# Light expert blocks: 512 columns of each full down slab multiplied in plain fp32 from the raw slot, the other 1536 split as before

## The chip, the core and the metric

The kernel runs on one core of one Trainium2 chip. The metric is the device time of one execution in microseconds (us), as the median of several runs. The engines that matter are TensorE (PE in the rows, PEld for its weight loads), VectorE (DVE), ScalarE (ACT), GpSimd (POOL), and SyncE (SP), whose queue issues the weight transfers.

## What is computed

A trunk of two encoder layers over 256 tokens of width 1024, all in float32. Each layer has a mixer (Hyena convolutions and differential attention) and a feed-forward part. The feed-forward part of layer 0 is a dense SwiGLU. That of layer 1 is a mixture of 8 experts of which each token uses 2:

```
def swiglu(x, w_gate, w_up, w_down):
    return (jax.nn.silu(x @ w_gate) * (x @ w_up)) @ w_down      # 1024 -> 2752 -> 1024

def moe_ffn(x, w_router, w_gate, w_up, w_down):
    logits = (xt @ w_router)
    top_val, top_idx = lax.top_k(logits, 2)
    ...                                    # tokens grouped by expert
    out = zeros.at[tok].add(expert_output * softmax(top_val))
```

The change touches the experts' `@ w_down` alone.

## The kernel before

Every weight is streamed from HBM once, in slabs of 128 partitions x 2048 float32 (1 MiB, 1.0486 MB). A slab passes through a pipeline. **SP** loads it into one of 6 raw slots (`RAW`). **ScalarE** copies it to `HI`, rounded to the reduced format float32r (line 768, `w_hi<-raw`). **VectorE** subtracts `HI` from the raw slab, which gives the remainder `LO` (line 1154, `w_lo<-raw,w_hi`). **TensorE** multiplies with `HI` and with `LO`, so that the sum is nearly a full float32 product. `HI` and `LO` have 3 slots each. The semaphores are `raw_loaded`, `hi_ready`, `lo_ready` and `slab_used`, each counting slabs in order. ScalarE splits slab n only when TensorE has used slab n-3. SP's queue is strictly in order: before each load it waits on `lo_ready` for the slab that had the same raw slot (line 591, in `put`), since after the subtraction nobody reads the raw slot any more.

The mixture of experts runs as blocks, one per expert, of 36 slabs each: slabs 0 to 3 are half slabs of gate and up weights (loaded in pairs), then come triples of two gate/up slabs and one down slab. Slabs 6, 9, ..., 33 are the full down slabs of a block, ten of them. Slabs 31 and 32 have 1536 columns, 34 has 1024 and 35 has 512. Blocks 0, 1, 3, 5 and 7 are heavy: up to 96 tokens, three multiplications for each piece of weight (high tokens by `HI`, low tokens by `HI`, high tokens by `LO`; lines 1723, 1724, 1990, 2013). Blocks 2, 4 and 6 are light: up to 64 tokens, of which the high part and the remainder stand side by side as 128 columns of the stationary operand, so that two multiplications do (lines 2069 and 2075 for gate/up, 2100 and 2107 for down). The rows 64 to 127 of the result then hold the product of the token remainders; `lo_copy` (line 1004) and `add_lo` (line 2081) bring them to the other rows.

In a light block each triple runs so. ScalarE: `turned_hi_light` (line 1016, the turned activations of the last chunk to float32r), split of the first slab, `lo_copy`, split of the second, `silu`, split of the down slab. VectorE: subtraction of the first slab, `mult_light` (line 1535, the product `act`), subtraction of the second, `turned_lo_light` (line 1545, the remainder of the activations), subtraction of the down slab. TensorE: gate/up slab, the transposes of `act` (`turn_act_light`, line 2088), gate/up slab, `down_light`, `add_lo`.

## Time and profile before

| what | value |
|---|---|
| median of 3 runs | 1379.55 us (1376.91 to 1380.21) |
| the profiled execution's own time | 1375.47 us |
| its span | 1373.6 us |
| granted TensorE clock, mean share of full speed | 0.998 |
| TensorE, VectorE, ScalarE busy | 95%, 83%, 64% of the span |
| read from HBM | 376.36 MB |

The profile is of one execution. Busy time is that of recorded instructions; a matmul's record covers its whole passage through the array, and records of successive matmuls overlap, so the distance between starts is the cost of one in a series. In a table of stretches the columns are the stretch and its length, then busy us of PE, PEld, DVE, ACT and POOL, the granted clock, the DMA share (mean busy share of 16 DMA engines) and GB/s. The mixture of experts fills the second half of the span, from about 640 us on; its three light blocks lie at about 840 to 922, 1015 to 1096 and 1187 to 1270 us.

### The profile page before, as it was taken

To read this page: it belongs to the slowest core of one execution; us is meant where nothing else is said; L and a number is where in the kernel's file an instruction comes from. 1 tells how busy PE (TensorE), PEld (TensorE's weight loads), DVE (VectorE), ACT (ScalarE), POOL (GpSimd) and SP (SyncE) were. 2 spreads that over 40 slices of the span, in tenths; PEclk is the share of its full clock that TensorE was granted. 3 is DMA by queue.
4 is the path that set the end of the run, shared out by engine and by line. 5 is a ranking of instruction groups with operands and counts; after the bars stand their busy time and mean duration, and the time that the engine had idled before them with its cause. 6 is when DMAs were issued, how large, how long until landed. Compare 5 with 4: busy or idle time off the path is not lost.

```text
span 1373.6 us, 17422 instructions
## 1 busy us (share of the span) xinstructions
PE 1311.0 (95%) x6156; PEld 982.4 (72%) x6156; DVE 1143.5 (83%) x1233; ACT 878.1 (64%) x965; POOL 81.0 (6%) x64
## 2 busy tenths in 40 slices
PE   6999989999999999999999999999999999999998
PEld 3887768888887887678667676666766667666675
DVE  5988787654447989875998988999889998899998
ACT  4345644544434445635776777987779877798775
POOL 0011010000000020010051000000000000000400
PEclk9999999999999999999999999999999999999999
DMA  7444333975483344152899999999999999999996
GB/s 293 180 157 150 123 137 138 337 288 184 172 345 120 152 153 153 62 207 92 320 364 382 414 360 372 404 405 422 380 365 411 402 422 386 364 406 401 421 395 256
DMA packets 63564, 394.67 MB, mean 287 GB/s; under 512 B 6914, under 2 KB 7486, under 8 KB 23818
## 3 DMA queue, kind: packets, MB, share of 16 engines
q1 hardware_dynamic: 58778, 375.37, 70.2%
q10 hardware_dynamic: 2848, 11.53, 2.1%
q0 software_dynamic: 1872, 6.91, 1.5%
q8 instruction: 38, 0.62, 0.2%
q14 instruction: 28, 0.23, 0.0%
HBM read 376.36 MB, written 17.43 MB: 287 GB/s over the span
## 4 chain that ended last, share of the span: by engine, by line
PE 70%; DVE 21%; issue 5%; ACT 3%; DVEq 0%; DMA 0%; SPq 0%; POOL 0%; ACTq 0%
PE bank L1723 15%; PE bank L1724 15%; DVE w_lo L1154 14%; PE bank L2013 13%; PE bank L1990 9%; PE bank L1773 5%; ACT w_hi L768 2%; PE bank L1768 2%; PE bank L1894 2%; PE bank L1736 1%; DVE ys L1143 1%; PE bank L1887 1%; PE bank L2000 1%; DVE act L1535 1%; PE bank L2107 1%
## 5 line engine op out<-in xcount | busy, mean ns | idle before, releaser
L1154 DVE TENSOR_TENSOR w_lo<-raw,w_hi 128x2048 fp32r<-128x2048 f32 (+2 forms) x383 | 794.1, 2089 | 94.0 <-ACT w_hi L768 92.7
L768 ACT ACTIVATE w_hi<-raw 128x2048 fp32r<-128x2048 f32 (+2 forms) x383 | 669.4, 1755 | 131.2 <-PE bank L2013 58.5
L1723 PE MATMUL bank<-w_hi,hT_hi 128*128 128x512 f32 (+3 forms) x968 | 382.5, 395 | 2.8 <-DVE hT_lo L1143 1.8
L1724 PE MATMUL bank<-w_hi,hT_lo 128*128 128x512 f32 (+3 forms) x968 | 375.1, 388 | 0.0
L1723 PEld LDWEIGHTS bank<-w_hi,hT_hi 128*128 128x128 f32 (+1 forms) x968 | 170.2, 176 | 51.7 <-issue 4.8
L1724 PEld LDWEIGHTS bank<-w_hi,hT_lo 128*128 128x128 f32 (+1 forms) x968 | 170.3, 176 | 44.8 <-issue 1.0
L1990 PE MATMUL bank<-w_lo,hT_hi 128*96 128x512 f32 (+3 forms) x616 | 162.3, 388 | 0.8 <-DVE w_lo L1154 0.8
L1990 PEld LDWEIGHTS bank<-w_lo,hT_hi 128*96 128x96 f32 (+1 forms) x616 | 103.1, 169 | 37.4 <-DVE w_lo L1154 4.3
L1773 PE MATMUL bank<-w_lo,hT_hi 128*128 128x512 f32 x352 | 87.5, 391 | 0.0
L2075 PE MATMUL bank<-w_lo,hT_hi 128*128 128x512 f32 (+1 forms) x264 | 78.2, 414 | 9.1 <-DVE w_lo L1154 9.1
L967 ACT ACTIVATE act_hi<-bank 128x192 fp32r<-128x192 f32 (+1 forms) x66 | 24.7, 375 | 94.8 <-PE bank L2000 94.8
L2013 PE MATMUL bank<-w_hi,act_lo 128*96 128x512 f32 (+1 forms) x294 | 78.8, 394 | 1.9 <-DVE act_lo L1495 1.8
L2013 PE MATMUL bank<-w_hi,act_hi 128*96 128x512 f32 (+1 forms) x294 | 78.5, 393 | 0.8 <-ACT act_hi L967 0.8
L2013 PE MATMUL bank<-w_lo,act_hi 128*96 128x512 f32 (+1 forms) x294 | 78.0, 391 | 0.0
L1773 PEld LDWEIGHTS bank<-w_lo,hT_hi 128*128 128x128 f32 x352 | 65.8, 188 | 13.9 <-issue 0.4
L2069 PE MATMUL bank<-w_hi,hT_hi 128*128 128x512 f32 (+1 forms) x264 | 74.4, 400 | 0.2
L2075 PEld LDWEIGHTS bank<-w_lo,hT_hi 128*128 128x128 f32 x264 | 44.5, 188 | 36.5 <-DVE w_lo L1154 31.2
L2013 PEld LDWEIGHTS bank<-w_hi,act_lo 128*96 128x96 f32 (+1 forms) x294 | 48.8, 169 | 22.7 <-DVE act_lo L1495 6.4
L2013 PEld LDWEIGHTS bank<-w_lo,act_hi 128*96 128x96 f32 (+1 forms) x294 | 49.6, 169 | 17.7
L2013 PEld LDWEIGHTS bank<-w_hi,act_hi 128*96 128x96 f32 (+1 forms) x294 | 49.2, 169 | 17.4 <-issue 1.0
L2069 PEld LDWEIGHTS bank<-w_hi,hT_hi 128*128 128x128 f32 x264 | 46.9, 188 | 10.9 <-ACT w_hi L768 1.5
L1495 DVE TENSOR_TENSOR act_lo<-bank,act_hi 128x192 fp32r<-128x192 f32 (+1 forms) x66 | 26.9, 407 | 28.4 <-ACT act_hi L967 28.3
(281 smaller groups left out, 1347.9 us busy)
## 6 DMA issues: line engine op xcount, KB each, us to landing
raw<-in_moe SPq DMA_DIRECT2D x240, 1024.0 KB, 7.9
raw<-in_mix SPq DMA_DIRECT2D x56, 1024.0 KB, 4.9
raw<-in_dense SPq DMA_DIRECT2D x30, 1024.0 KB, 4.9
raw<-in_moe SPq DMA_DIRECT2D x16, 768.0 KB, 8.4
raw<-in_moe SPq DMA_DIRECT2D x12, 512.0 KB, 7.4
slot_h<-x_squared ACTq DMA_DIRECT2D x1, 5632.0 KB, 43.0
slot_y<-x_squared ACTq DMA_DIRECT2D x1, 5632.0 KB, 24.2
raw<-in_moe SPq DMA_DIRECT2D x8, 256.0 KB, 5.4
```

The lines of the kernel that those rows point to most:

```text
L768: nc.scalar.activation(HI[:, split_slot, 0:width], RAW[:, raw_slot, half:half + width], ACT.Copy)\
L1154: vec.tensor_tensor(LO[:, split_slot, 0:width], RAW[:, raw_slot, half:half + width], HI[:, split_slot, 0:width].bitcast(F32), ALU.subtract ...
L1495: vec.tensor_tensor(R["act_lo"][:, :, 0:tbs * rows], turn_bank(layer, parity)[:, 0:2 * tbs * rows].rearrange("p (k t) -> p k t", k=2), R[" ...
L1723: mm(out_, left[0], right[0], start=start, stop=False)
L1724: mm(out_, left[1], right[1], start=False, stop=False)
L1768: ins = mm(bank(step, m)[:, 0:T], w_lo, HTH[:, kd, :], start=False, stop=sp_)
L1773: ins = mm(bank(step, tb)[:, :], HTH[:, kd, tok], w_lo, start=False, stop=sp_)
L1894: ins = mm(dst[:, :], DFT[:, 0, ri, par, :], src, start=True, stop=True)
L1990: ins = mm(gate_up_bank(tb, parity)[0:rows, 0:2 * width], HTH[:, kd, tok], w_lo, start=False, stop=kd == KD - 1)
L2013: ins = mm(PS[4 + 2 * tb + half][0:rows, :], left[0:h, k, tok], right[0:h, s, at:at + 512], start=first and k == 0, stop=last and k == 1)
L2069: mm(PS[parity][:, 0:2 * width], HTH[:, k0 + k, 0:2 * LCAP], w_hi, start=k0 + k == 0, stop=False)
L2075: ins = mm(PS[parity][:, 0:2 * width], HTH[:, k0 + k, 0:2 * LCAP], w_lo, start=False, stop=k0 + k == KD - 1)
```

## The change

In light blocks the last 512 columns (1536 to 2047) of each full down slab are no longer split. ScalarE and VectorE split only the first 1536 (`SPLIT_PART`). TensorE multiplies the last 512 straight from the raw slot in plain float32, with an unsplit copy of the turned activations (`ACT_WHOLE`, 64 columns) that ScalarE now makes ahead of the float32r copy. In `down_light` three of the four pieces remain in the `HI` group and in the `LO` group; the plain multiplication stands behind the `HI` group, ahead of the wait for `lo_ready`. As TensorE now reads the raw slot too, SP waits on `slab_used` instead of `lo_ready` before it loads into a slot that held such a slab; this also holds where the next load is that of the following heavy block. Nothing changes in heavy blocks otherwise, and the transfers are the same in number, size and order.

```diff
 LIGHT = 3
+LIGHT_BLOCKS = tuple(2 * i + 2 for i in range(LIGHT))
 PAIR = CAP + LCAP
...
 LATE_SLAB = 19
+LIGHT_DOWN = range(6, 34, 3)
+SPLIT_PART = SLAB - 512
 REJOINED = (LATE_SLAB - 2 + RAW_SLOTS, LATE_SLAB - 1 + RAW_SLOTS)
...
     FSP = sb("filters", [P, 2, 2, 2, 512])
+    ACT_WHOLE = SQUARES[:, 0:LCAP]
     HG = FSP[:, 0].rearrange("p a b c -> p a (b c)")
...
     def _(sp):
-        def put(slot, dst, src, free):
+        def put(slot, dst, src, free, multiplied=False):
             if free is not None:
-                sp.wait_ge(lo_ready, free)
+                sp.wait_ge(slab_used if multiplied else lo_ready, free)
             sp.dma_start(dst, src).then_inc(raw_loaded[slot], 16)
+
+        def follows_whole(b, p, late=False):
+
+            before = p - back(p, late)
+            return isinstance(b, int) and before % FFN_SLABS in LIGHT_DOWN and b + before // FFN_SLABS in LIGHT_BLOCKS
...
-            def two_halves(e, b, p, n):
+            def two_halves(e, b, p, n, multiplied=False):
...
                 put(slot, RAW[:, slot, :].rearrange("p (h n) -> p h n", h=2),
-                    blocks[e, at].rearrange("o (h p n) -> p (o h) n", h=2, p=P), n - back(p % FFN_SLABS) + 1)
-
-            def slab(e, b, p, n, late):
+                    blocks[e, at].rearrange("o (h p n) -> p (o h) n", h=2, p=P), n - back(p % FFN_SLABS) + 1, multiplied)
+
+            def slab(e, b, p, n, late, multiplied=False):
...
                     put(slot, RAW[:, slot, cols], blocks[e, at].rearrange("o (p n) -> p (o n)", p=P)[:, cols],
-                        None if i else n - back(p, late) + 1)
+                        None if i else n - back(p, late) + 1, multiplied)
...
                 for p in (0, 2):
-                    two_halves(e, at, p, n0 + p)
+                    two_halves(e, at, p, n0 + p, layer == 1 and follows_whole(b, p))
                 for i in range(4):
                     for j in range(6):
-                        slab(e, at, 4 + 6 * i + j, n0 + 6 * i + 4 + j, at == NE - 1 and 4 + 6 * i + j >= LATE_SLAB)
+                        part = 4 + 6 * i + j
+                        late = at == NE - 1 and part >= LATE_SLAB
+                        slab(e, at, part, n0 + part, late, layer == 1 and follows_whole(b, part, late))
                     if i == 0 and (y_at or y_light_at):
...
                         sp.dma_start(TOK_HEAVY[0:tok_heavy_at[1], :], slot_h[bass.ds(*tok_heavy_at), :]).then_inc(tok_heavy_loaded, 16)
-                    slab(e, at, p, n0 + p, at == NE - 1)
+                    slab(e, at, p, n0 + p, at == NE - 1, layer == 1 and follows_whole(b, p, at == NE - 1))
...
-            def turned_hi_light(q):
+            def turned_hi_light(q, whole=True):
                 act.wait_ge(turned, q + 1)
+                if whole:
+                    nc.scalar.activation(ACT_WHOLE, PS[2][:, CAP:CAP + LCAP], ACT.Copy)
                 nc.scalar.activation(R["act_hi"][:, :, 0:LCAP], PS[2][:, 0:2 * CAP].rearrange("p (k t) -> p k t", k=2)[:, :, 0:LCAP], ACT.Copy)\
...
                 silu_light(qb, k0, 0)
-                ffn_split(6, b, n0, r0)
+                ffn_split(6, b, n0, r0, SPLIT_PART)
...
                     silu_light(q, k, parity)
-                    ffn_split(p + 5, b, n0, r0)
+                    ffn_split(p + 5, b, n0, r0, SPLIT_PART)
...
                 ffn_split(35, b, n0, r0, D // 2)
-                turned_hi_light(qb + NCH)
+                turned_hi_light(qb + NCH, False)
                 turned_tokens_hi(b + 1, CAP)
...
                 mult_light(qb, 0)
-                ffn_split(6, b, n0)
+                ffn_split(6, b, n0, SPLIT_PART)
                 turned_lo_light(qb)
...
                     turned_lo_light(q)
-                    ffn_split(p + 5, b, n0)
+                    ffn_split(p + 5, b, n0, SPLIT_PART)
...
-            def down_light(n, s, q, start, tiles=(0, 1), amid=None):
-
+            def down_light(n, s, q, start, tiles=(0, 1), amid=None, whole=None):
+
+                parts = [(j, k, half) for j, k in enumerate(tiles) for half in range(2)][:4 if whole is None else 3]
                 pe.wait_ge(act_hi_ready, q + 1)
...
                 pe.wait_ge(hi_ready, n + 1)
-                for j, k in enumerate(tiles):
-                    for half in range(2):
-                        at = j * D + half * 512
-                        mm(PS[4 + half][:, :], R["act_hi"][:, k, 0:2 * LCAP], HI[:, s, at:at + 512], start=start and k == 0, stop=False)
+                for j, k, half in parts:
+                    at = j * D + half * 512
+                    mm(PS[4 + half][:, :], R["act_hi"][:, k, 0:2 * LCAP], HI[:, s, at:at + 512], start=start and k == 0, stop=False)
+                if whole is not None:
+                    mm(PS[5][0:LCAP, :], ACT_WHOLE, RAW[:, whole % RAW_SLOTS, SPLIT_PART:SLAB], start=False, stop=False)
                 if amid:
...
                 pe.wait_ge(lo_ready, n + 1)
-                for j, k in enumerate(tiles):
-                    for half in range(2):
-                        at = j * D + half * 512
-                        ins = mm(PS[4 + half][:, :], R["act_hi"][:, k, 0:2 * LCAP], LO[:, s, at:at + 512], start=False, stop=False)
+                for j, k, half in parts:
+                    at = j * D + half * 512
+                    ins = mm(PS[4 + half][:, :], R["act_hi"][:, k, 0:2 * LCAP], LO[:, s, at:at + 512], start=False, stop=False)
                 ins.then_inc(slab_used, 1)
...
                             pe.wait_ge(y_taken, 2 * b + 2)
-                        down_light(n0 + p + 2, slot(p + 2), q - 1, opening)
+                        down_light(n0 + p + 2, slot(p + 2), q - 1, opening, whole=block_place(layer, b, p + 2))
                         add_lo(k0 + 1 + j, 1 - j)
...
                 gate_up_light(n0 + 29, slot(29), 4, 4, CHUNK, 1)
-                down_light(n0 + 30, slot(30), q - 1, False)
+                down_light(n0 + 30, slot(30), q - 1, False, whole=block_place(layer, b, 30))
                 add_lo(k0 + NCH - 1, 1)
...
                 gate_up_light(n0 + 32, slot(32), 4, 4, TAIL, 0)
-                down_light(n0 + 33, slot(33), q, False, amid=lambda: add_lo(k0 + NCH, 0, TAIL))
+                down_light(n0 + 33, slot(33), q, False, amid=lambda: add_lo(k0 + NCH, 0, TAIL),
+                           whole=block_place(layer, b, 33))
                 turn_act_light(q + 1)
...
                 down_light(n0 + 34, slot(34), q + 1, False, tiles=(0,))
```

## Rows read from the trace of the kernel before

**Rows 1.** The page, busy us, share of the span and instructions of each engine.

```profile
PE 1311.0 (95%) x6156; PEld 982.4 (72%) x6156; DVE 1143.5 (83%) x1233; ACT 878.1 (64%) x965; POOL 81.0 (6%) x64
```

**Rows 2.** Stretches of blocks 2, 6 and 3; busy us, clock, DMA share, GB/s.

```profile
868.00:889.00 21.00, 19.52 (x81) 13.55 (x80) 21.00 (x16) 19.87 (x19) 0.00 (x0) 1.00 1.01 423
1237.00:1258.00 21.00, 19.45 (x80) 13.44 (x79) 21.00 (x16) 19.77 (x18) 0.00 (x0) 1.00 1.01 421
945.00:966.00 21.00, 21.00 (x96) 14.79 (x95) 18.80 (x14) 14.99 (x14) 0.00 (x0) 1.00 1.01 421
```

**Rows 3.** VectorE in order of time, block 2: start us, us, instruction.

```profile
866.29 4.48 DVE L1154 TENSOR_TENSOR w_lo<-raw,w_hi 128x2048 fp32r<-128x2048 f32 x2
870.69 0.41 DVE L1535 TENSOR_TENSOR act<-silu,bank 64x256 f32<-64x256 f32 x1
871.02 2.28 DVE L1154 TENSOR_TENSOR w_lo<-raw,w_hi 128x2048 fp32r<-128x2048 f32 x1
873.23 0.28 DVE L1545 TENSOR_TENSOR act_hi<-bank,act_hi 128x128 fp32r<-128x128 f32 x1
873.43 4.48 DVE L1154 TENSOR_TENSOR w_lo<-raw,w_hi 128x2048 fp32r<-128x2048 f32 x2
```

**Rows 4.** ScalarE in order of time, block 2.

```profile
872.22 0.28 ACT L1016 ACTIVATE act_hi<-bank 128x128 fp32r<-128x128 f32 x1
...
908.45 0.25 ACT L1016 ACTIVATE act_hi<-bank 128x128 fp32r<-128x128 f32 x1
```

**Rows 5.** ScalarE's waits from 886 to 911 us: total us, times, longest.

```profile
ACT w_hi L768 <- DMA raw<-in_moe: 0.8, 2, 0.4
```

**Rows 6.** Groups by form, the whole span: count, busy us, mean ns.

```profile
L1154 DVE TENSOR_TENSOR w_lo<-raw,w_hi 128x2048 fp32r<-128x2048 f32 x308 | 699.2, 2285 | 79.7 <-ACT w_hi L768 78.9
...
L1154 DVE TENSOR_TENSOR w_lo<-raw,w_hi 128x1536 fp32r<-128x1536 f32 x18 | 31.5, 1752 | 4.3 <-ACT w_hi L768 4.3
...
L768 ACT ACTIVATE w_hi<-raw 128x2048 fp32r<-128x2048 f32 x308 | 587.8, 1913 | 127.2 <-PE bank L2013 57.5 <-PE bank L1773 42.3 <-PE bank L1768 23.5
...
L768 ACT ACTIVATE w_hi<-raw 128x1536 fp32r<-128x1536 f32 x18 | 26.7, 1482 | 0.1
```

**Rows 7.** TensorE at slab 30 of block 2, in order of time.

```profile
910.28 1.08 PE L2100 MATMUL bank<-w_hi,act_hi 128*128 128x512 f32 x4
911.64 1.19 PE L2107 MATMUL bank<-w_lo,act_hi 128*128 128x512 f32 x4 [0.28 <-DVE w_lo L1154]
912.67 0.39 PE L2081 MATMUL bank<-lo_sum,swap 128*128 128x512 f32 x1
```

**Rows 8.** Plain float32 matmuls at the end of the span.

```profile
1366.26 3.67 PE L2234 MATMUL bank<-y_spread,spread_T 96*128 96x512 f32 x8 [0.78 <-ACT y_spread L1115]
```

**Rows 9.** VectorE, then TensorE, at slab 6 of block 2.

```profile
850.78 2.28 DVE L1154 TENSOR_TENSOR w_lo<-raw,w_hi 128x2048 fp32r<-128x2048 f32 x1
...
854.52 1.07 PE L2107 MATMUL bank<-w_lo,act_hi 128*128 128x512 f32 x4
```

**Rows 10.** Single loads: issue, us to landing; slabs 12, 13, 14, block 6's first.

```profile
L591 SPq DMA_DIRECT2D raw<-in_moe x1: 333/333/333, 853.2 to 853.2; - x1
DMA to landing us min/median/max: 6.8/6.8/6.8
...
L591 SPq DMA_DIRECT2D raw<-in_moe x1: 332/332/332, 855.9 to 855.9; - x1
DMA to landing us min/median/max: 6.6/6.6/6.6
...
L591 SPq DMA_DIRECT2D raw<-in_moe x1: 333/333/333, 859.2 to 859.2; - x1
DMA to landing us min/median/max: 7.4/7.4/7.4
...
L591 SPq DMA_DIRECT2D raw<-in_moe x1: 397/397/397, 1175.1 to 1175.1; - x1
DMA to landing us min/median/max: 5.0/5.0/5.0
```

## The prediction

> **What bounds the kernel now.** Start with the busy shares of the page [rows 1]: TensorE 95% and VectorE 83% of the span. These are averages over stages, so the second view is the table of stretches [rows 2]. It shows two regimes inside the expert stage. In a heavy block TensorE is busy 21.00 of 21.00 us while VectorE has 18.80. In a light block it is the other way round: VectorE is busy for 21.00 or almost 21.00 us of 21, TensorE for about 19.5. All three stretches have one thing in common, a DMA share of 1.01 at 421 to 423 GB/s, whether the block consumes quickly or slowly. One slab is 1.0486 MB, so at 422.5 GB/s, about the middle, a slab lands every 2.48 us and three slabs take 7.45 us.
>
> The third view is VectorE in order of time in the first light block [rows 3]. One period of three slabs (gate/up, gate/up, down) starts with a w_lo subtraction at 866.29 and ends with the next at 873.43: 7.14 us. From start to start the two subtractions take 4.40 us (2.20 each), the product `act` 0.33, the third subtraction 2.21 and the remainder of the token copy 0.20: 7.14 again. So VectorE runs without a gap, and this is what the change shortens. But 7.14 us is less than the 7.45 that the transfers need: the light block already eats the ring of raw slots faster than it is filled, 0.31 us per period. The ring's lead is gone before the block ends: at 886 to 911 us ScalarE, which splits first, waits for landings (0.8 us in two waits of 0.4) [rows 5]. In the last third of a light block transfers and VectorE are level, and behind the transfers there is nothing to win.
>
> **The change part by part.** *Subtraction.* A down slab of 2048 columns costs 2.21 us, one of 1536 columns 1.752 against 2.285 in single durations [rows 6]: 0.53 less, 10 slabs in 3 blocks, 16.0 us of VectorE time. A period would go from 7.14 to 6.61 us if VectorE set it. The transfers need 7.45. So this gain is spent on the ring running out earlier (0.84 us per period instead of 0.31), and what survives is only the distance between the last landings and the end of the block.
>
> *ScalarE.* The copy to w_hi goes from 1.913 to 1.482 us [rows 6], minus 0.43. The new copy ACT_WHOLE (128x64) has no row; the token copy of 128x128 takes 0.25 to 0.28 [rows 4], so it is between 0 and 0.28; I take 0.2, near that row, for half its columns. The period of ScalarE falls by some 0.2 and stays below 7.45. Cost nothing; if the transfers did not cover it, 30 x 0.2 = 6 us, less the 13 that the shorter copies give.
>
> *TensorE.* Per down slab one w_hi and one w_lo multiplication of 512 columns go, and a plain fp32 one comes. Four fp32r ones from 910.28 to 1.08 us later, each 0.39 long, are 0.23 apart [rows 7]. Eight records of plain fp32 of 512 columns take 3.67 us with 0.59 for the last one [rows 8]: 0.44 apart, and one fp32 matmul of the code leaves two records (four calls, eight records). So plain fp32 costs 0.88 against 2 x 0.23 = 0.46: TensorE gets 0.42 us of work per down slab. A period has 19.5/21 of busy time by the records [rows 2], but it waits for w_lo in each group, so there is room for the sum. Where it stands matters: the fp32 matmul lies before `lo_ready`. Now the w_hi group of slab 30 starts at 910.28 and the w_lo group at 911.64, 1.36 later, when the subtraction is done [rows 7]. After: three of 0.23 plus 0.88 = 1.57, so w_lo can't start before 911.85; three instead of four save 0.23 behind it, and `add_lo` at 912.67 comes at about 912.5. The subtraction is 0.53 sooner, but TensorE takes back some 0.3. At the end of a light block I count 0.33 gained, 1.0 for three; the bounds are 0 (TensorE takes back all) and 1.1 per block (the last two down slabs, nothing taken back), 3.2 in all.
>
> *The slots.* Ten raw slots of a light block are released by `slab_used` instead of `lo_ready`, and SP waits in order. In the middle of a block this is about 0.9 us later (three w_lo matmuls and their end, 1.2 us for four [rows 7]) less the 0.53: harmless, since loads already take 6.6 to 7.4 us around slab 12 [rows 10] and more when the ring's lead is used up, so that several are queued. At the opening it is not small. The subtraction of slab 6 is done at 853.06, SP issues slab 12 at 853.2 [rows 9, 10]. TensorE finishes slab 6 only at 854.52 + 1.07 = 855.59 [rows 9]. The new w_hi group starts 0.53 sooner and lasts 0.65 longer, the w_lo group is 0.23 shorter, so slab 12 is issued at about 855.6, 2.4 later. Slab 12 landed at 853.2 + 6.8 = 860.0 [rows 10], the one before it a spacing earlier, 857.5. The lead of issue over the previous landing falls from 4.3 to 1.9 us. What lead is enough? Lower bound: the shortest latency of such a load in these rows is 5.0 us [rows 10], minus 2.5 of transfer, a lead of 2.5; then a hole of 0.6. Upper bound: slab 14, issued at 859.2, landed at 866.6, 4.1 after slab 13 (855.9 + 6.6 = 862.5) [rows 10]. It had a lead of 3.3 and still left a hole of 1.6, so a lead of 4.9 is needed; then slab 12 leaves 3.0. Slabs 12 and 13 are loaded before that old hole of 1.6, which takes up a delay of that size, as slab 14 is released by slab 8 as before. What comes through is 0 to 1.4 us per block. I take the middle, 0.7, and 2.1 for three blocks; nothing behind hides it, because the rest of the block is at the transfer rate.
>
> The Trainium skill ("DMA: Bandwidth & Descriptors", Latency and other measured facts) puts the fixed cost of a DMA at about 2 us. By it the hole would be about 0.1 instead of 0.6 to 3.0, and the sum would fall below zero by the 1.0 gained; the 1.6 hole of slab 14 does not fit it.
>
> The same page (Where 436 GB/s comes from) puts the ceiling at 435 GB/s. By it three slabs would take 7.23 us, still more than 6.61, and each of some ten periods would have 0.2 us more to give; the trace never shows more than 423 in these stretches.
>
> *Heavy blocks behind.* Slab 30 gates the next block's first load the same way, up to 1 us later. TensorE sets the pace there, 21.00 of 21.00 us, with VectorE 2.2 us in hand over the stretch [rows 2], so I cost it at nothing; uncovered it would be 3 x 1 us. Arithmetic and volume of transfers are otherwise unchanged.
>
> Sum: -1.0 + 2.1 = +1.1 us on the profiled execution's 1375.47 (span 1373.6): 1376.6. The median of the runs is 4.08 above that execution, so 1380.6.
>
> **The rivals.** *VectorE is the bound throughout*: its gapless row speaks for it, the share of 1.01 and ScalarE's waits for landings against. 30 x 0.53 = 16.0 us, 1363.6. Chance 0.06.
>
> *The transfers lose their holes*: if the 1.6 us hole at slab 14 comes from VectorE being late and not from the queue, a faster VectorE closes it in three blocks: 4.8 + 1.0 = 5.8 us less, 1373.8. For it speaks that slab 14's load waits for the late subtraction of slab 8; against it, that a lead of 3.3 us is more than the 2.5 of the shortest load. Chance 0.15.
>
> *Slower, through the late release at the opening*: lead 1.9 us at slab 12. If 4.9 is needed and the old hole at slab 14 does not absorb (it moves along), 3.0 per block, 9.0 in all less 1.0 gained: 1387.6. With absorption and no gain at the end, +4.2. It decides from a needed lead of some 4.5 us on. Chance 0.23 for over 0.3%.
>
> *Nothing measurable* (the forecast's case, -3 to +4 us): 0.56.
>
> **How the numbers follow.** 0.3%, 4.1 us, is about what a measurement of this kernel can tell from no change. Faster: 0.06 + 0.15 = 0.21; same 0.56; slower 0.23. The likeliest case's own range is 1377 to 1384. Taking in the closed holes and most of the late release gives 1373 to 1387, with some 0.2 outside: the full VectorE gain, the full 9 us, and what I have not seen.
>
> **What would show it.** Right: w_lo of the down slabs 1.75 us, DMA share still 1.0 at some 422 GB/s in the middle of light blocks, VectorE now with gaps there, and more waits of ScalarE for landings, and from the middle of the block on instead of its last third; there periods of 7.45 us. Right for the slots: slab 12 of a light block issued 2.4 us later, with a slower landing. Wrong: periods of 6.6 us through the block, or more than 430 GB/s; or, on the other side, waits of TensorE in the heavy blocks, or the granted clock falling below 1.00 in light blocks [rows 2].

## The result and the profile after

The changed kernel takes 1385.26 us (median of 8 runs, 1382.05 to 1386.98). The kernel before, run beside it, takes 1379.88 (median of 8; one of them took 1846.83 us and is left out of the ratio; the others have a median of 1379.55). The ratio is 1.0042 with a 95% interval of 1.0030 to 1.0053: **slower by 0.42%, 5.8 us**. It lies inside the range of 1373 to 1387, but outside the likeliest case's own range of 1377 to 1384, and it has the sign and size of the slower rival. The profiled execution took 1385.68 us, span 1383.8.

Ratios below are against the kernel before, run on the same chip; 0.001 is 1.38 us, and each ratio is uncertain by 0.001 to 0.002.

The page, in the form of [rows 1]:

```profile
PE 1328.7 (96%) x6156; PEld 982.8 (71%) x6156; DVE 1129.1 (82%) x1233; ACT 872.1 (63%) x995; POOL 80.4 (6%) x64
```

VectorE lost 14.4 us of work and TensorE gained 17.7. The stretch of block 2 answers to [rows 2]:

```profile
868.00:889.00 21.00, 20.56 (x81) 13.19 (x80) 19.62 (x16) 18.98 (x22) 0.00 (x0) 1.00 0.99 400
```

The clock is still 1.00. TensorE is now busy for 20.56 us of 21 where it had 19.52, and VectorE, gapless before, has 19.62. VectorE in order of time, block 2, beside [rows 3]:

```profile
867.24 2.28 DVE L1167 TENSOR_TENSOR w_lo<-raw,w_hi 128x2048 fp32r<-128x2048 f32 x1
...
869.64 3.94 DVE L1167 TENSOR_TENSOR w_lo<-raw,w_hi 128x1536 fp32r<-128x1536 f32 x2
874.05 0.41 DVE L1548 TENSOR_TENSOR act<-silu,bank 64x256 f32<-64x256 f32 x1 [0.46 <-ACT silu L1022]
874.39 2.28 DVE L1167 TENSOR_TENSOR w_lo<-raw,w_hi 128x2048 fp32r<-128x2048 f32 x1
```

The two subtractions went from 4.48 to 3.94 us, the 0.53 that was promised. But from 867.24 to 874.39 the period is 7.15 us, where it was 7.14: the time came back as a gap of 0.46 us before `act`, waiting for `silu`. Nothing of the saving is left, and that already at 870 us, where transfers don't yet hold anything back. The chain of waits says who holds it:

```profile
867.24 2.29 DVE w_lo L1167
...
869.57 1.21 PE bank L2088 x4
870.78 0.69 PE bank L2113 x3
871.48 1.00 PE bank L2115 x2
872.48 0.89 PE bank L2121 x3
873.37 0.24 PE bank L2094
...
873.64 0.39 ACT silu L1022
...
874.05 0.06 DVE act L1548
874.10 0.28 issue
874.39 2.29 DVE w_lo L1167
```

This is a closed loop, and each turn is one period: the w_lo subtraction of a gate/up slab, its w_lo matmuls (L2088), the down slab's w_hi matmuls (L2113), the plain multiply (L2115, 1.00 us), the down slab's w_lo matmuls (L2121), `add_lo` (L2094), `silu`, `act`, and the next subtraction. Before the change the same loop held two more float32r matmuls of 0.23 us [rows 7] and no plain multiply, so it was about 7.15 - 1.00 + 0.46 = 6.6 us long, half a microsecond under the 7.14 of VectorE, and didn't show.

The forms answer to [rows 6] and [rows 8]:

```profile
L1167 DVE TENSOR_TENSOR w_lo<-raw,w_hi 128x1536 fp32r<-128x1536 f32 x48 | 83.5, 1745 | 4.3 <-ACT w_hi L779 4.3
...
L2115 PE MATMUL bank<-raw,squares 128*64 128x512 f32 x60 | 32.2, 618 | 0.0
```

ScalarE's waits for landings, 886 to 911 us, beside [rows 5]:

```profile
ACT w_hi L779 <- DMA raw<-in_moe: 2.2, 3, 1.0
```

The loads of slabs 12, 14 and 18 of block 2 (issue, us to landing; the first two answer to [rows 10]), and then slab 18 before the change:

```profile
L595 SPq DMA_DIRECT2D raw<-in_moe x1: 333/333/333, 859.2 to 859.2; - x1
DMA to landing us min/median/max: 4.8/4.8/4.8
...
L595 SPq DMA_DIRECT2D raw<-in_moe x1: 333/333/333, 862.6 to 862.6; - x1
DMA to landing us min/median/max: 6.4/6.4/6.4
...
L595 SPq DMA_DIRECT2D raw<-in_moe x1: 333/333/333, 873.5 to 873.5; - x1
DMA to landing us min/median/max: 7.3/7.3/7.3
```

```profile
L591 SPq DMA_DIRECT2D raw<-in_moe x1: 333/333/333, 868.7 to 868.7; - x1
DMA to landing us min/median/max: 7.8/7.8/7.8
```

Read them against the block's own start. VectorE's subtraction of slab 6 starts at 854.03 after and at 850.78 before [rows 9], so the profiled block begins 3.25 us later. The code ahead of it is the same; at least part of this is TensorE's clock, which was granted at its lower level (0.50, 1.2 GHz) for 6.8 us each from 184.3 and from 426.7 us on in the execution after, and for 3.4 us each from 424.8 and from 643.3 on in the one before. Less 3.25, slab 12 is issued at 855.95 (before 853.2: 2.75 late) and lands at 860.75 (860.0: 0.75 late). Slab 14 lands at 865.75 (866.6: 0.85 early). Slab 18 is issued at 870.25 (868.7: 1.55 late) and lands at 877.55 (876.5: 1.05 late). So the delay at the opening is swallowed by the old hole at slab 14, and a new one arises at slab 18, in the middle of the block. From the end of slab 12's subtraction to the issue of slab 18's load there are 2.15 us, where there were 0.17. Measured from slab 6's subtraction, slab 24 lands 0.86, 1.44 and 1.16 us later than before in the three blocks: 3.5 us together.

**Where the time is lost in the trace.** The light blocks can be timed by themselves, from VectorE's subtraction of slab 6 to that of slab 4 of the next block. For block 2 the first line is the end of that stretch before (its start is in [rows 9]), the others are its start and end after:

```profile
927.98 2.29 DVE L1154 TENSOR_TENSOR w_lo<-raw,w_hi 128x2048 fp32r<-128x2048 f32 x1
```

```profile
854.03 1.74 DVE L1167 TENSOR_TENSOR w_lo<-raw,w_hi 128x1536 fp32r<-128x1536 f32 x1
...
933.20 2.29 DVE L1167 TENSOR_TENSOR w_lo<-raw,w_hi 128x2048 fp32r<-128x2048 f32 x1
```

That is 77.2 us before and 79.2 after; the three blocks together take 231.3 and 238.1, 6.7 more. The two stretches between them, each nearly a whole heavy block, take 97.1 us before and after. Of the 6.7 us, 2.7 are lost at the ends of the blocks: from the subtraction of slab 30 to that of the next block's slab 4 it takes 19.56, 19.57 and 19.66 us where it took 18.66, 18.66 and 18.75. The largest step there is from slab 33's subtraction to slab 34's, 3.8 us instead of 2.8.

### The profile page after: what moved, and what is told of

Read it like the earlier page. It is cut to its first block, busy times and chain, and to the rows that moved or that the text cites. A ratio compares the mean times of both kernels' runs of the same rounds, so it can differ in the third digit from the quotient of the medians.

```text
span 1383.8 us, 17452 instructions
## 1 busy us (share of the span) xinstructions
PE 1328.7 (96%) x6156; PEld 982.8 (71%) x6156; DVE 1129.1 (82%) x1233; ACT 872.1 (63%) x995; POOL 80.4 (6%) x64
## 4 chain that ended last, share of the span: by engine, by line
PE 75%; DVE 15%; ACT 5%; issue 3%; DMA 1%; SPq 0%; POOL 0%; DVEq 0%; ACTq 0%
PE bank L1736 15%; PE bank L1737 15%; PE bank L2026 13%; DVE w_lo L1167 9%; PE bank L2003 8%; PE bank L1786 5%; ACT w_hi L779 3%; PE bank L2088 3%; PE bank L1781 2%; PE bank L1749 2%; PE bank L1907 1%; DVE ys L1156 1%; DMA raw<-in_moe 1%; PE bank L2115 1%; PE bank L1900 1%
## 5 line engine op out<-in xcount | busy, mean ns | idle before, releaser
L1167 DVE TENSOR_TENSOR w_lo<-raw,w_hi 128x2048 fp32r<-128x2048 f32 (+2 forms) x383 | 778.7, 2047 | 97.2 <-ACT w_hi L779 95.5
L779 ACT ACTIVATE w_hi<-raw 128x2048 fp32r<-128x2048 f32 (+2 forms) x383 | 657.4, 1722 | 141.0 <-PE bank L2026 56.4
L2088 PE MATMUL bank<-w_lo,hT_hi 128*128 128x512 f32 (+1 forms) x264 | 75.9, 405 | 10.8 <-DVE w_lo L1167 9.6
L2088 PEld LDWEIGHTS bank<-w_lo,hT_hi 128*128 128x128 f32 x264 | 46.0, 188 | 34.4 <-DVE w_lo L1167 27.5
L2026 PEld LDWEIGHTS bank<-w_lo,act_hi 128*96 128x96 f32 (+1 forms) x294 | 49.6, 169 | 17.7
```

The costliest lines, as they stand in the source:

```text
L779: nc.scalar.activation(HI[:, split_slot, 0:width], RAW[:, raw_slot, half:half + width], ACT.Copy)\
L1167: vec.tensor_tensor(LO[:, split_slot, 0:width], RAW[:, raw_slot, half:half + width], HI[:, split_slot, 0:width].bitcast(F32), ALU.subtract ...
L2026: ins = mm(PS[4 + 2 * tb + half][0:rows, :], left[0:h, k, tok], right[0:h, s, at:at + 512], start=first and k == 0, stop=last and k == 1)
L2088: ins = mm(PS[parity][:, 0:2 * width], HTH[:, k0 + k, 0:2 * LCAP], w_lo, start=False, stop=k0 + k == KD - 1)
```

## The experiments

**The change in four parts.** Four kernels make a square: with and without the shorter split, the plain multiply and the late release. In `late_release_alone` the arithmetic is that of before and only SP's wait is changed. In `early_release` the plain multiply reads a resident tile instead of the raw slot, so the slot is free at `lo_ready`; the product is of other data. `no_plain_multiply` and `split_less_alone` leave the product over the last 512 columns of the light blocks' down slabs out.

```diff
# late_release_alone, in the kernel before (with follows_whole as in the change)
-                sp.wait_ge(lo_ready, free)
+                sp.wait_ge(slab_used if multiplied else lo_ready, free)
# early_release, in the changed kernel
-                sp.wait_ge(slab_used if multiplied else lo_ready, free)
+                sp.wait_ge(lo_ready, free)
-                    mm(PS[5][0:LCAP, :], ACT_WHOLE, RAW[:, whole % RAW_SLOTS, SPLIT_PART:SLAB], start=False, stop=False)
+                    mm(PS[5][0:LCAP, :], ACT_WHOLE, X[:, 0, 0:512], start=False, stop=False)
# no_plain_multiply: the line mm(PS[5]...) taken out
# split_less_alone: that, and sp.wait_ge(lo_ready, free)
```

> The kernel before, in which only SP's waits for the ten down slabs of each light block are changed from lo_ready to slab_used; no column is treated differently, the output is unchanged. Theory A (the late release leaves holes in the transfers) expects +3 to +6 us against the kernel before, holes at slab 12, at slab 18 and at the next block's first load, and later landings at the end of light blocks. Theory B (the cost is the plain multiplication in TensorE's chain) expects within 1 us of the kernel before. If VectorE's saving matters at all, this one is slower than the changed kernel.

> The changed kernel, with SP waiting on lo_ready as before; so that this is free of races, the plain multiplication reads 512 columns of the residual stream instead of the raw slot (512 columns of each full down product in light blocks are therefore of other data). Same instructions and sizes on every engine. Theory A: most of the loss is gone, -1 to +2 us against the kernel before; what stays is the tail of light blocks, where slab 34 comes 0.9 us later per block. Theory B: +4.5 to +6, as the changed kernel.

> The changed kernel without the plain fp32 multiplication (512 columns of each full down slab of light blocks are left out of the product); the late release stays, but slab_used comes 0.9 us sooner. Theory A: the lead at slab 12 is 0.9 us longer, so about half of the holes stay, +1 to +3 us against the kernel before. Theory B: the loss is gone, -3 to 0.

> The changed kernel with neither the plain multiplication nor the late release (512 columns of each full down slab of light blocks are left out of the product). It shows what 16 us less of VectorE and 13 us less of ScalarE are worth by themselves. If the transfers bound the light blocks as forecast, -1 to -4 us against the kernel before. If VectorE bounds them, -12 to -16 us.

| kernel | split cut | plain multiply | late release | ratio (95%) | us |
|---|---|---|---|---|---|
| late_release_alone | no | no | yes | 1.0024 (1.0012 to 1.0036) | +3.3 |
| early_release | yes | yes | no | 1.0018 (1.0008 to 1.0028) | +2.5 |
| no_plain_multiply | yes | no | yes | 0.9982 (0.9969 to 0.9994) | -2.5 |
| split_less_alone | yes | no | no | 0.9957 (0.9942 to 0.9972) | -5.9 |
| the change | yes | yes | yes | 1.0042 (1.0030 to 1.0053) | +5.8 |

By these ratios the parts add up. Late release: +3.3 alone, 5.8 - 2.5 = +3.3 with the plain multiply, -2.5 + 5.9 = +3.4 without it. Plain multiply: 2.5 + 5.9 = +8.4 with the early release, 5.8 + 2.5 = +8.3 with the late one. Shorter split: -5.9. Sum: -5.9 + 8.4 + 3.3 = +5.8.

Against what was expected: `late_release_alone` is within theory A's +3 to +6. `early_release` lies between A's -1 to +2 and B's +4.5 to +6, since each theory held one of two causes for the whole. `no_plain_multiply` is within B's -3 to 0, and `split_less_alone` lies between the -1 to -4 for transfers as the bound and the -12 to -16 for VectorE.

The three light blocks in the profiled executions (one each; the three blocks of the kernel before agree within 0.2 us) give the same order, but smaller sizes for two parts:

| kernel | three light blocks, us | against before |
|---|---|---|
| before | 231.3 | 0 |
| late_release_alone | 236.6 | +5.3 |
| early_release | 234.4 | +3.1 |
| no_plain_multiply | 231.7 | +0.4 |
| split_less_alone | 228.3 | -3.0 |
| the change | 238.1 | +6.7 |

The shorter split is worth 3.0 us here, not 5.9, and the plain multiply costs 6.1 to 6.3, not 8.4. Part of the gap is TensorE's clock in other stages: the six runs of `split_less_alone` had a mean granted clock of 0.9968, the 29 of the kernel before beside them 0.9948, and over all runs of the kernel before that are on record a run is about 0.9 us shorter for each 0.001 more. By this estimate some 2 us of the 5.9 have nothing to do with the edit. The late release costs 3.4 to 3.7 us in the two pairs with the shorter split. Alone it shows 5.3, of which 2.8 stand between slabs 6 and 12 of blocks 2 and 6; there the clock was granted at 0.50 (1.2 GHz) for 3.4 us, from 856.2 and from 1207.8 on, after TensorE had been busy for 3.45 of 6.2 us and for 3.88 of 6.8. Without these 2.8 it is 2.5.

With neither the plain multiply nor the late release the period is 6.87 us, not the 6.61 that VectorE alone would allow. VectorE of `split_less_alone` in order of time, then ScalarE:

```profile
867.03 2.27 DVE L1167 TENSOR_TENSOR w_lo<-raw,w_hi 128x2048 fp32r<-128x2048 f32 x1
...
873.56 0.41 DVE L1548 TENSOR_TENSOR act<-silu,bank 64x256 f32<-64x256 f32 x1 [0.19 <-ACT silu L1022]
873.90 2.28 DVE L1167 TENSOR_TENSOR w_lo<-raw,w_hi 128x2048 fp32r<-128x2048 f32 x1
```

```profile
870.59 0.59 ACT L1015 ACTIVATE lo_sum<-bank 64x512 fp32r<-64x512 f32 x1 [0.42 <-PE bank L2088]
871.21 1.92 ACT L779 ACTIVATE w_hi<-raw 128x2048 fp32r<-128x2048 f32 x1
```

This is a second loop. The subtraction that starts at 867.03 feeds four matmuls, ScalarE's `lo_copy` waits 0.42 us for them (870.59), then comes a whole w_hi copy (1.92), then `silu`, `act` at 873.56 and the next such subtraction at 873.90. It is 6.87 us long, so 0.27 of VectorE's 0.53 can't come out.

**Where the plain multiply stands.** `own_semaphore` gives the plain multiply a semaphore of its own, so that SP needn't wait for the w_lo group behind it. `plain_between_groups` also moves it ahead, between the w_hi and the w_lo group of the gate/up slab before (at a block's first down slab it stays). `plain_after_add` moves it behind `add_lo` instead, in the eight middle down slabs of each block; the first and the last are split whole.

```diff
# own_semaphore
-                sp.wait_ge(slab_used if multiplied else lo_ready, free)
+                sp.wait_ge(lo_ready, free)
+                if multiplied:
+                    sp.wait_ge(whole_used, multiplied)
...
+                        .then_inc(whole_used, 1)
# plain_between_groups, beside that: passed to gate_up_light as amid
+            def whole_between(n, q, place):
+                pe.wait_ge(act_hi_ready, q + 1)
+                pe.wait_ge(hi_ready, n + 1)
+                down_whole(place)
# plain_after_add, beside that
                         add_lo(k0 + 1 + j, 1 - j)
+                        if not opening:
+                            down_whole(block_place(layer, b, p + 2))
```

> The changed kernel, with the late release mended and the output intact: the plain multiplication counts a semaphore of its own, and SP waits on lo_ready and on that one instead of slab_used. As the multiplication stands before the w_lo group, it is over when the subtraction is or up to 0.9 us later. If late release and plain multiplication add up, as in the runs so far, +2 to +3.5 us against the kernel before, like the run with early release. Rival: the release was not what counted there but the other data read by TensorE (the raw slot is being read while transfers write next to it); then +5 to +6.

> As own_semaphore, and the plain multiplication moves ahead: between the w_hi and the w_lo group of the gate/up slab before, where TensorE waits 0.2 to 0.5 us for VectorE (the first down slab of each block stays as it is). If the cost of the plain multiplication is that it lies in the loop w_lo of gate/up, w_hi of down, plain, w_lo of down, add_lo, silu, act, subtraction (7.13 us in the changed kernel's chain, 6.2 without the plain one), the period falls to about 6.9 us until the transfers run out, and the time to -3 to -6 us against the kernel before, close to the run without the plain multiplication. If the cost is TensorE's work as such, it stays at +2 to +3.

> The plain multiply of a down slab is issued behind the addition of the low part instead of ahead of it, with a semaphore of its own for the slot's release, in the eight middle slabs of each light block; slabs 6 and 33 are split whole as before the change. If the loop through the addition and silu is what the multiply lengthens, it is now out of it: the period falls towards the 6.87 us of the kernel without the multiply, and the time is 1 to 4 us under the kernel before. If the slot's later release (about 1.8 us behind the split) costs what that takes back, 0 to +3 us.

`own_semaphore`: 1.0044 (1.0030 to 1.0057), the time of the change itself. Nothing came back that can be measured. The multiply that reads the slot is itself late: slab 18's load is issued 1.29 us after slab 12's subtraction has ended, against 2.15 in the change and 0.17 before. The expected +2 to +3.5 missed, and the +6.1 is what the expectation gave to its rival, that TensorE's reading of the raw slot costs and not the release. This run can't tell the two apart. Against the rival stand the multiply's mean record, 618 ns both from the raw slot and from the resident tile of `early_release`, and `late_release_alone`, where no multiply reads the slot and the release costs all the same.

`plain_between_groups`: 1.0008 (0.9998 to 1.0019), 4.7 us under the change and level with before. Both expectations missed: +1.1 us lies between the -3 to -6 for a cost by the loop and the +2 to +3 for a cost by TensorE's work as such. ScalarE's waits for landings are short now, 0.5, 0.6 and 0.2 us in the three light blocks. Releasing early pays. In the trace its light blocks take 231.6 us, 2.8 fewer than those of `early_release`, and the gain stands at the ends of the blocks (18.46 us from slab 30 in block 2, against 19.57); in the middle six slabs take 14.20 against 14.25, a period of 7.10. There its TensorE has hardly any time left:

```profile
889.00:910.00 21.00, 20.92 (x82) 13.22 (x81) 19.61 (x15) 18.78 (x22) 0.00 (x0) 1.00 1.01 420
```

and its chain shows the multiply in the second loop, ahead of the w_lo matmuls for which `lo_copy` waits:

```profile
876.19 1.00 PE bank L2112 x2
877.19 1.14 PE bank L2093 x4
...
878.35 0.02 ACT lo_sum L1020
```

`plain_after_add`: 1.0048 (1.0029 to 1.0067), +6.6 us, and both expectations for it missed. TensorE is busy for 20.87 of 21 us from 868 to 889. Its chain shows what is queued behind the multiply: the next gate/up slab's two groups, then the transposes for which ScalarE waits with `act_hi`:

```profile
877.32 1.00 PE bank L2112 x2
878.32 1.13 PE bank L2087 x4
879.45 0.93 PE bank L2093 x4
880.38 0.18 PE bank L2106 x2
```

The period there is 6.87 us in places, but the slot comes free later still, and ScalarE waits for landings for 2.7, 3.0 and 2.1 us in the three blocks. How its 6.6 us divide between the two isn't measured, and its eight runs had a lower mean granted clock (0.9939) than the 17 of the kernel before beside them (0.9956).

**A dose of the suspect.** `plain_twice` issues each plain multiply twice, so that this product counts double.

```diff
                     mm(PS[5][0:LCAP, :], ACT_WHOLE, RAW[:, whole % RAW_SLOTS, SPLIT_PART:SLAB], start=False, stop=False)
+                    mm(PS[5][0:LCAP, :], ACT_WHOLE, RAW[:, whole % RAW_SLOTS, SPLIT_PART:SLAB], start=False, stop=False)
```

> The changed kernel with each plain multiply issued twice, so that the product over those 512 columns is counted double. If the period of a light block goes through TensorE's work ahead of the addition (multiply, addition, silu, act, next split), each extra multiply of 0.9 to 1.0 us shows in full where the slab lies in that loop: the period of 7.13 us rises to about 8.0, above the 7.45 us of three slabs' transfers, and the time by 20 to 27 us over the changed kernel. If TensorE has idle time there to take it, or transfers hold the period, at most +3 us at the tails of the three blocks.

The time is 1405.24 us, ratio 1.0202 (1.0180 to 1.0224): 0.0160 or 22 us over the change. Its VectorE in order of time:

```profile
866.33 2.28 DVE L1167 TENSOR_TENSOR w_lo<-raw,w_hi 128x2048 fp32r<-128x2048 f32 x1
...
873.98 0.41 DVE L1548 TENSOR_TENSOR act<-silu,bank 64x256 f32<-64x256 f32 x1 [1.30 <-ACT silu L1022]
874.32 2.28 DVE L1167 TENSOR_TENSOR w_lo<-raw,w_hi 128x2048 fp32r<-128x2048 f32 x1
```

The period is 7.99 us: 0.84 more than the change's 7.15, all of it in the wait for `silu`, which grew from 0.46 to 1.30. The second multiply is 0.86 us long on its chain, so in this loop TensorE's work costs what it takes. The expected 20 to 27 us over the change came. Ten times 0.84 in three blocks would be 25; 22 came.

**Transfers out of the way.** In three kernels SP loads only the first half of each slab of the light blocks that is loaded singly (all but the first four), so that half their columns are stale. The kernels are before, the change, and `split_less_alone`.

```diff
                     cols = slice(i * width // pieces, (i + 1) * width // pieces)
+                    if layer == 1 and b in (2, 4, 6):
+                        cols = slice(0, width // 2)
```

> The kernel before, but the slabs 4 to 35 of the light blocks are loaded only by their first half of columns (the other half keeps what the slot held, so the light experts' products are of other data). Everything else runs as before, so the transfers can't bound a light block. If they bound only its last third and the beginning of the heavy block behind, -1 to -4 us against the kernel before: VectorE's 7.14 us per period stay.

> The changed kernel with the same half loads (same remark on its products). If the late release costs through holes in the transfers, it costs nothing here, and this run is +1.5 to +3 us above half_loads_before, by the 0.9 us at the tail of each light block, the period of 7.13 us being the same. If the saving of VectorE was only hidden by the transfers, as I forecast, it comes out here: 10 to 15 us below half_loads_before.

> The kernel with neither the plain multiply nor the late release, with half of each slab loaded, so that the transfers can't set the period; the product is of partly stale weights. If ScalarE's loop (low copy, split, silu, act, next split) holds 6.87 us with transfers idle, the time is that of the same kernel with full loads, less what the tails give, -6 to -9 us against the kernel before. If transfers held it and VectorE is next, the saving of 0.53 us of 30 periods comes out in full, -14 to -17 us.

| with half loads | ratio (95%) | us | the same with full loads |
|---|---|---|---|
| before | 0.9994 (0.9984 to 1.0004) | -0.8 | 0 |
| the change | 1.0019 (1.0010 to 1.0028) | +2.6 | +5.8 |
| split_less_alone | 0.9931 (0.9914 to 0.9949) | -9.5 | -5.9 |

The stretch of `half_loads_before` shows a DMA share of 0.63 and VectorE still full:

```profile
889.00:910.00 21.00, 19.50 (x81) 13.51 (x80) 21.00 (x16) 19.78 (x19) 0.00 (x0) 1.00 0.63 201
```

So with the transfers a third idle the kernel before gains 0.8 us, which is within the noise of nothing (its light blocks take 231.0 us in the trace instead of 231.3): VectorE bounded it, not the transfers. The change is still 3.4 us slower than that. The shorter split gains 9.5 - 0.8 = 8.7 us of the 16.0, since the loop of 6.87 us stays: from 7.14 the difference is 0.27 us, and some nine periods in three blocks give 7.3. In the trace the light blocks of the three kernels take 231.0, 234.1 and 223.5 us: 7.5 for the shorter split, 10.6 for the multiply. `half_loads_after` had foreseen +1.5 to +3 over `half_loads_before` if no transfer counts; 3.4 by the ratios, 3.1 in the trace.

The two other kernels show where the multiply costs when nothing else is in the way. First `half_loads_after`, then `half_loads_split_less`, VectorE's products at the start and the end of block 2:

```profile
861.04 0.41 DVE L1550 TENSOR_TENSOR act<-silu,bank 64x256 f32<-64x256 f32 x1 [0.67 <-ACT silu L1024]
...
918.12 0.41 DVE L1550 TENSOR_TENSOR act<-silu,bank 64x256 f32<-64x256 f32 x1 [0.99 <-ACT silu L1024]
...
923.72 0.35 DVE L1550 TENSOR_TENSOR act<-silu,bank 64x192 f32<-64x192 f32 x1 [1.65 <-ACT silu L1024]
```

```profile
857.10 0.41 DVE L1550 TENSOR_TENSOR act<-silu,bank 64x256 f32<-64x256 f32 x1 [0.67 <-ACT silu L1024]
...
911.69 0.41 DVE L1550 TENSOR_TENSOR act<-silu,bank 64x256 f32<-64x256 f32 x1 [0.31 <-ACT silu L1024]
...
916.20 0.35 DVE L1550 TENSOR_TENSOR act<-silu,bank 64x192 f32<-64x192 f32 x1 [0.57 <-ACT silu L1024]
```

Over the eight periods the first takes 57.08 us and the second 54.59: 2.5 more. The last stretch, where slab 33's multiply stands ahead of the last `add_lo`, takes 5.60 against 4.51: 1.1 more. That is 3.6 us per block and 10.7 in three, of the 12.1 measured between the two (1.0019 - 0.9931). With full loads 6.1 to 6.3 of it shows in the trace (8.4 by the ratios). That waits for landings overlap the waits for TensorE there would explain it; it wasn't tested.

**The opening alone.** `first_down_slab_as_before` splits slab 6 of each light block whole and releases it as before; the nine other down slabs stay changed.

```diff
-LIGHT_DOWN = range(6, 34, 3)
+LIGHT_DOWN = range(9, 34, 3)
```

> The changed kernel, but the first down slab of each light block (slab 6) is split whole, as before the change, and frees its slot as before; the nine others stay changed. It removes the late release at the opening of a block (slab 12's load issued at its old time) and nothing else. If the opening is the place of the loss, as the prediction named it (lead fallen from 4.3 us, 0.7 us each block and more with the following slabs), 2 to 4 us of the 5.4 come back: +1.5 to +3.5 us against the kernel before. If the late releases at slabs 15 and 18 and at the next block's first load cost as much, and most of the loss is TensorE's own work, 0 to 2 us come back: +3.5 to +5.5 us.

1.0044 (1.0028 to 1.0060), +6.1 us: nothing of the 5.8 us came back, and even the higher of the two expected ranges ended at +5.5. Slab 12's load is issued at 856.0; those of slabs 17 and 18:

```profile
L595 SPq DMA_DIRECT2D raw<-in_moe x1: 333/333/333, 869.2 to 869.2; - x1
DMA to landing us min/median/max: 7.9/7.9/7.9
...
L595 SPq DMA_DIRECT2D raw<-in_moe x1: 333/333/333, 873.1 to 873.1; - x1
DMA to landing us min/median/max: 8.0/8.0/8.0
```

Its slab 6 is subtracted at 853.57, 2.79 later than before [rows 9]. Less that, slab 12 is issued at 853.2, as before, but slab 18 at 870.3, 1.6 late, and it lands at 878.3, 1.8 later than before. Slab 17 lands at 877.1, so slab 18 follows by 4.0 us instead of 2.48, though it was issued 4.0 us ahead of that landing. The delay at slab 18 stands here without the delay at the opening.

But its hole of 1.5 us is no empty queue. While slab 18 was on its way there was a stretch in which the DMA engines were busy and moved little. In the change, while the late slab 12 was due, they were idle for most of a microsecond. The last three numbers are the granted clock, the DMA share and GB/s:

```profile
875.00:876.00 1.00, 1.00 (x6) 0.57 (x4) 1.00 (x1) 0.82 (x3) 0.00 (x0) 1.00 0.97 229
```

```profile
859.00:860.00 1.00, 1.00 (x6) 0.83 (x5) 0.33 (x2) 0.98 (x3) 0.00 (x0) 1.00 0.37 156
```

## Why the prediction was right or wrong

- **Durations, right.** Subtraction 1.745 us (1.752 foreseen), `ACT_WHOLE` 0.214 (0.2, its 30 copies in the trace after). The plain multiply takes 1.00 us on the chain, against 0.88 estimated from [rows 8].
- **"Behind the transfers there is nothing to win": wrong.** The step took 7.45 us of transfers against 7.14 of VectorE as the bound. But the ring's lead carries 0.31 us per period nearly through the block; with the transfers a third idle the kernel before gained 0.8 us. The shorter split is worth 3.0 us in the trace and 5.9 by the ratios, not 1.0. Of the 16.0 us of VectorE work, 8.5 (16.0 - 7.5) stay out in the trace with the transfers a third idle, where the loop of 6.87 us through `lo_copy` holds, and 4.5 (7.5 - 3.0) go to the transfers; by the ratios 7.3 and 2.8. My main reason for the missing gain was the smaller of the two.
- **TensorE, "there is room for the sum": this is the step that failed.** I summed busy time over a period, and looked at order only at slab 30. The multiply stands in a closed loop that had 0.5 us to spare and was lengthened by 0.54, in a kernel whose other loops had become shorter. It costs 6.1 to 6.3 us in the trace and 8.4 by the ratios (10.6 and 12.1 with the transfers out of the way, two thirds of it in the loop and a third at the ends of the blocks). I had it take back 0.3 of the 0.53 us at slab 30 and counted a gain of 0.33 per block at the end. Measured there is a loss of 0.9 per block, most of it at slab 33, which I didn't look at.
- **The slots, about right in size, wrong in place.** Predicted +2.1 at the opening and "harmless" in the middle; measured +3.3. Slab 12 was issued 2.75 us late (2.4 foreseen) and landed 0.75 late (0.6 to 3.0 foreseen), but the hole at slab 14 took that up and undoing it brought nothing back. What was called harmless was not: TensorE ends a down slab later relative to VectorE than I reckoned, since VectorE, held by the loop, is no longer earlier. Slab 18 is issued 1.55 us late instead of 0.9 - 0.53. The lead of up to 4.9 us that a load was said to need was read from a hole that a short lead didn't make: in the change slab 15, issued 2.6 us ahead of slab 14's landing, lands 2.9 after it, a hole of 0.4 where slab 14 with its lead of 3.3 had left 1.6.
- **Heavy blocks, right.** Costed at nothing; in the trace the stretches from slab 4 of block 3 and of block 5 to slab 6 of the light block behind take 97.11 and 97.08 us before, 97.07 and 97.07 after.
- **The number.** 1380.6 came from -1.0 + 2.1. The parts are -5.9 + 8.4 + 3.3 by the ratios and -3.0 + 6.1 + 3.7 in the trace. Two terms that I put at nearly nothing, the worth of the shorter split and TensorE's cost, are large and of opposite sign, so that the range held was luck. The rival "slower through the late release at the opening" (0.23) had the sign and nearly the size, but its mechanism, the late release, explains little over half, and its place is refuted for the change as made. "The transfers lose their holes" and "VectorE is the bound throughout" are refuted for the change as made; the second was nearer to the truth of the kernel before than the forecast was.

The Trainium skill's fixed cost of about 2 us per DMA ("DMA: Bandwidth & Descriptors", Latency and other measured facts) would ask for a lead of about as much, an estimate from that figure. The trace agrees where a load found the queue nearly empty. In `plain_twice` slab 12, issued 0.1 us ahead of the previous landing, lands 4.7 us after it, 2.2 more than the 2.48 of a transfer; slab 15, with a lead of 1.8, lands 2.9 after it, 0.4 more. The holes at slab 14 before and at slab 18 in `first_down_slab_as_before` don't speak against that figure, as the prediction took the first to do; they have another cause, which stays open.

No version beat the kernel before with the whole computation in it; the best, `plain_between_groups`, is level with it.

## What to carry to other kernels

Work moved off a full engine is worth no more than the distance to the next tightest closed loop. Follow the loops across engines (subtraction, matmuls, addition, activation, product, and back) and write down the length of each: here 7.14, 6.87 and 6.6 us stood side by side, and the 0.53 us saved on the first met the second after 0.27. Work that is added is priced by the loop it enters, not by the engine's idle share: 0.54 us more in the loop of 6.6 gave back what had been won. Look at the ends of a block apart from its middle: there the multiply was a loss outright. A transfer rate that is nominally short binds only once the ring's lead is used up; halve the loads to see whether it does. Where an effect is 3 us in 1380, time the changed stage in the trace as well, since the granted clock in other stages moves the whole by 2.

## What was unexpected

- The three parts add to within 0.1 us of the whole (-5.9, +8.4, +3.3 against +5.8), though each ratio is uncertain by 1.4 to 2 us, and the trace has two of them over 2 us smaller. The sum doesn't vouch for its terms: an error in `split_less_alone` enters twice, with opposite signs.
- A late load is not punished where it is first late. The existing hole behind slab 12 absorbs it; six slabs on, where there was none, a load issued 4.0 us before the previous landing still left 1.5 us, with 8.0 us to landing, while slab 12 of the change landed 4.8 us after its issue. The DMA engines were busy in that hole and moved 229 GB/s. Why stays open.
- A separate semaphore for the reader of the slot changed nothing measurable (1.0044 against 1.0042), since the reader itself was late.
